# A two-block transformer step on one core: every product whose sum nobody reads is left out

## Chip, cores and metric

The kernel is one program on one core of a Trainium2 chip. The metric is the device time of one execution in microseconds, from three executions of the kernel before. The five engines of the core are TensorE (PE, with its weight loads PEld), VectorE (DVE), ScalarE (ACT), GpSimd (POOL) and SyncE (SP), which issues the weight loads from memory. Activations between the stages stay in SBUF; the weights, about 305 MB, are read once.

## What is computed

A sequence of 256 rows of width 1024 goes through two blocks of two layers each, all in float32. Cut to what matters:

```python
# first block: two layers
for layer in range(2):
    x = x + 0.5 * swiglu(rms_norm(x), w_gate, w_up, w_down)            # f0, f2
    h = rms_norm(x, mix_norm[layer])
    x = x + (diff_stickbreak_mixer(h) if layer == 0 else mla_mixer(h))  # m0, m1
    x = x + memory_cross_attention(rms_norm(x), rms_norm(mem))          # c0, c1
    x = x + 0.5 * swiglu(rms_norm(x), w_gate, w_up, w_down)            # f1, f3
# second block: two layers
for l in range(2):
    h = x @ w_in[l]
    mix = concat([gla(h), rwkv7(h), nsa(h)]) @ w_out[l]
    x = layer_norm(ALPHA * x + mix)                                     # b0, b1
    x = layer_norm(ALPHA * x + swiglu(x))                               # f4, f5
```

None of the products that the change leaves out appears in this text. They multiply the 128x128 identity by itself, and their sums are overwritten unread.

## The kernel before

The work is cut into twelve stages that run one after the other: `f0 m0 c0 f1 f2 m1 c1 f3 b0 f4 b1 f5` (`STAGES`). The `f` stages are feed-forward layers, `m0` and `m1` the two mixers of the first block, `c0` and `c1` its cross attentions, `b0` and `b1` the mixers of the second block. In the trace `m0` and `c0` lie about between 205 and 450 us, `m1` and `c1` between 822 and 1070, `b0` between 1240 and 1560, `b1` between 1755 and 2080; what lies between these stretches is feed-forward.

Every stage is a list of pieces. A piece has a name and a number, and each engine has a function that does its part of it, so the list of pieces is the order of the work on all engines alike. Each engine runs its part in that order and waits on semaphores where it needs another engine's result. In an `f` stage the list is written by a few loops. In the six other stages (`m0 c0 m1 c1 b0 b1`) it is woven from chains: a chain is a list of pieces that follow each other, each chain has a letter, and the string of the stage in the table `WEAVE` (line 40) says letter by letter from which chain the next piece comes (`woven`, line 1204).

The letter `z` is one chain more. Its pieces are called "warm", and TensorE alone does them. The code is (lines 334 and 3092)

```python
    def idle_banks(self, pe):
        return [self.ps[b] for b, key in self.holder.items() if pe.knows(*self.at("evicted", key))]

def pe_warm(e, K):
    for b in K.idle_banks(e)[0:1]:
        e.mm(b[:, 0:128], K.ident, K.ident, True, True, free=True)
```

So a warm piece is one float32 product of the identity (tile `consts`) with itself, 128x128 by 128x128, into a bank of PSUM whose last content TensorE knows to be read already. It waits for nothing and signals nothing. Where no bank is known to be free it is nothing at all: the strings have 1009 `z`, and the program has 955 such products. A float32 product of this size is two rows MATMUL and two LDWEIGHTS in the trace, so the group `ps<-consts 128*128 128x128` with 1912 rows is these 955 products and one more.

What else the prediction's steps touch:

- Weights come in units of up to 1024 columns. SP loads a unit into one of six places of `ring`. ACT copies it to `w_hi` (`act_splits`, the value rounded to float32r), DVE writes the rest to `w_lo` (`dve_splits`), and TensorE multiplies with both. There are four places for such pairs; ACT waits until TensorE has used the pair before.
- Activations are split in the same way: `h` holds hi and lo halves, and `x` is the residual stream.
- A linear layer (`pe_lin`) is a run of products `ps<-w_hi,h` and `ps<-w_lo,h`, or `ps<-h,w_hi` and `ps<-h,w_lo` in the feed-forward layers.
- At the end of a stage the parts of `x` are finished one by one: DVE adds the sum, ACT and DVE split it into the next stage's `h` (`act_x`, `dve_x`), POOL squares it and adds the squares in `rows` (`pool_x`). TensorE's first linear layer of the next stage waits for the parts in turn, and in its middle for POOL's squares (`pe_rs`, products `ps<-consts,rows`).
- Head norms are chains on DVE: a reduction, some fifteen small operations on `stats`, and the multiplications (`act_head_squares`, `dve_head_norm`). TensorE then turns the result (`tr`, line 145, `ps<-consts,scratch`).

Of the kernel before, what the change touches and what calls it, by code (L numbers as in the profile page):

```python
# [37 lines left out]


WEAVE = {  # L40
    "b0": ("zzzzzzzzzrzzrrrrrgzgzgrhlzhzhzzzzrzzzhzzzzzzzrzzhrzzzhzgzzhzzzzzzzhzzzzzzzzhzzhzzzzzzzzzzrzzzzzz"
           "zzzzhhrhzzzzzzzhzzzzzzlzhzzzzhzrrrzzhzrlhzhzzrrzszzzhzrzsrzzzhzzzsszhzzzzzszzszzzzznzzzzzzzzzzrz"
           "rzzzzzzzzsrnznzrzzzzzzrznzzzzzzzznnnzzzzzzzzzznzzwzzzzzzzzzzzzzzzzzzzzzrzzzzzzzzzzzzzzzzvrsvrrnz"
           "zzzzzzrzzrnrnzrzzzzzzzzzzzrwzzrurnrsunsuwvsrsbsusrvrrruzvbrvrarvrwbabuwurwaawrauramurzvzwbuabzbv"
           "awzzbumabummzmzzzmmmmmmmzmmmmzzzzzzzzzzzmmzzmzmmmmmmzmzmzmzzmzzzzzzzzmzzzmzzzzzmmmmzzzz"),
    "b1": ("zzzzzzzzzzrzrrgrzgrgrhgzzrrlhzzzzzzzzzzzzzzzzzzzzzhhzzzrzzzrzzhhzzhzzzzzzzzzzzzzzzzzzzzzzzzzzzzz"
           "zzzzzzzzzzzzzrhhhzzrzzhzzhzzzzzzlzzzrzzrzzzzzzzzzzzrrhhzrshzzhzsrzzlsszhrhszzrhzrrhrzhsrhzzzzzzz"
           "zzszrzzzzszrzzznrzszzzzzznzrsnrzzznzznzzzzzznrrrnwzzzzzzzzzzzzzzzzzzzzzzznzzzzzzzzzzruzzzzzzzzzz"
           "zzzzzzzzzzzzzzzzzrsrwnzrznzszzszzrsrzzrrnzrrnrnrzurvrwwbuavrrvmrvzzrvzzzzazbubvwbauawwuaubwvauab"
           "buvuwvazbuambummmzzzzmzmmmmmmzmzzzzmmmzmmmmmmmmzzzzmzzzmzzzzzmzmzzmzmzzzzmzzzzmzmzzzzmzzm"),  # L50
    "c0": ("zzzzzzzzzpppzzzzpzzzzzzzzzzzzzzzzzzzzzzzzzzzzzzzzzzzzzzzzzzzpzpazcbacdbzacdbdozozzzozoozoozzozoo"
           "zzzzzzozozzzzzzzzzzzozzzzzzzzz"),
    "c1": ("zzzzzpppzzzpzzzzzzzzzzzzzzzzzzzzzzzzzzzzzzzzzzzzzzzzzzppazbdazbcdabcdcozzoozozozzooozozzzoozzzzz"
           "zzzzzzzzzzzzzzzoozzzz"),
    "m0": ("zzypzzzzzqqzzzzzqzzzzzzzzkzkqzzpzzzzzzzzzzzzzzzzkyzzzzzzykbakyqlycvaycvbaabcacbcaacctbsbatscaacc"
           "tassactszczssotzystzztssyzzzootsttotstoozzozzzzzzzzozzoozozoozoozzzzzozoozzzzzz"),
    "m1": ("zyzpzzzzzqqzqzkkqzyzqyzzkzqqzqkzzzqkzzzzzzzzzzzzzzzzzzzzzzzzzzzzzzzzkzzzzzzzzzzzzzzzzzzzzzzzzzzz"
           "zzzzzzzzzzzzzkzzzzzzhzzzzzzzzzzzzzzzzzyzzzzzzzyzttzzttzzzzyztzzzzzzzzzttztzzzzzzzzzzzzzuzuzyuayu"
           "zuucauducbadacbedacbedbacaebcodaceabcbedadebecdzaobedaeoozozzzozoozoooooozozzzzozozzzzzzzzzzzzzz"
           "z"),  # L60
}

# [3170 lines left out]
```

How the kernel before makes its waits and increments, by code:

```python
    def wait_ge(self, sem, n):  # L114
        if self.e is not None and self.covered.get(id(sem), 0) < n:
            self.e.wait_ge(sem, n)
            self.covered[id(sem)] = n
# [8 lines left out]
    def then(self, ins, kind=None, key=None):  # L126
        if kind is None:
            self.n_own += 1
            sem, n = self.K.S.sem(self.own), self.n_own
            ins.then_inc(sem, 1)
        else:
            ins.then_inc(*self.up(kind, key))
            sem, n = self.K.S.at(kind, key)
        self.wait_ge(sem, n)
# [187 lines left out]
    def bank(self, pe, ring, key):  # L323
        i = self.cursor.get(ring, 0)
        self.cursor[ring] = i + 1
        b = ring[i % len(ring)]
        if b in self.holder:
            pe.wait_ge(*self.at("evicted", self.holder[b]))
        self.holder[b] = key
        self.where[key] = b
        return self.ps[b]
# [43 lines left out]
def act_splits(e, K):  # L376
    while e.next_split < len(K.pairs):
        u = K.pairs[e.next_split]
        before = K.pairs[u.pair - NU] if u.pair >= NU else None
        if u.piece > e.piece + 1 and not can_split(e, K, u, before):
            return
        assert before is None or before.piece <= e.piece, (u.n, u.piece, e.piece)
        if before is not None:
            e.wait_ge(*K.used(before))
        e.wait_ge(*K.loaded(u))
        e.act(u.his, u.src, ACT.Copy).then_inc(*e.up("split_hi", u.n))
        e.next_split += 1
# [2 lines left out]
def dve_splits(e, K):  # L391
# [5 lines left out]
            return  # L397
        if before is not None:
            e.wait_ge(*K.used(before))
        e.wait_ge(*K.loaded(u))
```

## Time and profile before

| | |
|---|---|
| runs of the kernel before | 2283.53, 2286.56, 2306.3 us |
| median | 2286.56 us |
| span of the profiled execution | 2285.3 us |
| instructions in the span | 36711 |
| TensorE busy | 2202.2 us, 96% |
| VectorE busy | 1526.7 us, 67% |
| ScalarE busy | 1104.3 us, 48% |
| GpSimd busy | 418.3 us, 18% |
| mean granted TensorE clock | 0.988 |

The span is the time from the first to the last instruction of one profiled execution. The page gives no other time for that execution; the span is 1.3 us under the median. Busy is the time in which an engine has at least one instruction in work. The end of a product on TensorE is modelled and laps over the start of the next by some 0.2 us, so a run of equal products is measured best from its start to the start of what follows it. The granted clock is 1.00 where TensorE runs at 2.4 GHz and 0.50 at 1.2 GHz.

### The profile page before, as it was taken

How to read it: one execution, taken by the hardware profiler on the slowest of the kernel's cores; microseconds unless marked ns; L12 is line 12 of the kernel's file. 1: busy time of each engine (PE TensorE's matmuls, PEld its weight loads, DVE VectorE, ACT ScalarE, POOL GpSimd, SP SyncE). 2: the span in 40 equal slices, each digit the busy share in tenths (PEclk: the TensorE clock that was granted, in tenths of full speed). 3: DMA queues.
4: the chain of work that ended last, by engine and by line, in shares of the span. 5: the costliest groups of instructions: out<-in, count | busy, mean ns of one | idle time of the engine just before them, and what ended most of it. 6: DMA issues, size and time to landing. Idle time of an engine off the chain costs nothing.

```text
span 2285.3 us, 36711 instructions
## 1 busy us (share of the span) xinstructions
PE 2202.2 (96%) x14388; PEld 1953.8 (85%) x14388; DVE 1526.7 (67%) x2709; ACT 1104.3 (48%) x1997; POOL 418.3 (18%) x379
## 2 busy tenths in 40 slices
PE   6999999999999999999999998999998999999997
PEld 5888888988888888999888987889887988788886
DVE  5976765587678667756876685456766586456765
ACT  4654454365456544535654522346555432345554
POOL 2521001122112100012220030101213123101223
PEclk9999999999999999999999999999999999999999
DMA  6545432254555443133544321114544320303552
GB/s 242 192 170 173 148 130 74 74 192 182 180 194 190 177 157 133 38 111 130 188 179 174 139 85 61 57 38 152 186 181 149 133 94 1 116 29 127 187 178 90
DMA packets 88444, 310.32 MB, mean 136 GB/s; under 512 B 9808, under 2 KB 11600, under 8 KB 87760
## 3 DMA queue, kind: packets, MB, share of 16 engines
q1 hardware_dynamic: 87984, 305.29, 37.5%
q8 instruction: 114, 1.87, 0.3%
q10 hardware_dynamic: 288, 2.69, 0.3%
q14 instruction: 58, 0.48, 0.1%
HBM read 306.89 MB, written 1.05 MB: 135 GB/s over the span
## 4 chain that ended last, share of the span: by engine, by line
PE 91%; DVE 4%; ACT 2%; DMA 1%; issue 1%; POOL 0%; SPq 0%; DVEq 0%; ACTq 0%; POOLq 0%
PE ps L140 89%; PE ps L145 2%; DVE scratch L165 2%; DMA ring<-in_w 1%; ACT w_hi L154 1%; DVE w_lo L165 1%; ACT scratch L154 0%; DVE x L165 0%; DVE scratch L192 0%; DVE stats L182 0%; POOL scratch L165 0%; ACT scratch L191 0%; DVE scratch L177 0%; DVE scratch L171 0%; SPq L207 0%
## 5 line engine op out<-in xcount | busy, mean ns | idle before, releaser
L165 DVE TENSOR_TENSOR w_lo<-ring,w_hi 128x1024 fp32r<-128x1024 f32 (+2 forms) x571 | 694.2, 1230 | 420.0 <-ACT w_hi L154 414.3
L140 PE MATMUL ps<-h,w_hi 128*128 128x512 f32 (+1 forms) x2784 | 872.2, 372 | 24.0 <-DVE h L177 19.1
L154 ACT ACTIVATE w_hi<-ring 128x1024 fp32r<-128x1024 f32 (+2 forms) x571 | 581.5, 1032 | 487.0 <-PE ps L140 485.4
L140 PE MATMUL ps<-h,w_lo 128*128 128x256 f32 x2448 | 688.0, 281 | 0.0
L140 PEld LDWEIGHTS ps<-h,w_hi 128*128 128x128 f32 x2784 | 504.2, 190 | 123.3 <-issue 21.4
L140 PEld LDWEIGHTS ps<-h,w_lo 128*128 128x128 f32 x2448 | 465.0, 190 | 0.0
L140 PE MATMUL ps<-f,w_hi 128*128 128x512 f32 (+1 forms) x1444 | 419.2, 356 | 3.2 <-DVE f L165 3.2
L140 PE MATMUL ps<-f,w_lo 128*128 128x256 f32 x1184 | 331.9, 280 | 0.0
L165 POOL TENSOR_TENSOR f<-f_work,f 128x256 fp32r<-128x256 f32 x132 | 187.7, 1422 | 596.2 <-ACT f L154 596.1
L140 PEld LDWEIGHTS ps<-f,w_hi 128*128 128x128 f32 x1444 | 254.4, 189 | 46.1 <-DVE w_lo L165 3.6
L140 PE MATMUL ps<-scratch 128*128 128x128 f32 (+9 forms) x1952 | 256.3, 300 | 8.7 <-DVE scratch L192 2.5
L140 PE MATMUL ps<-consts 128*128 128x128 f32 x1912 | 246.5, 280 | 0.0
L140 PEld LDWEIGHTS ps<-consts 128*128 128x128 f32 x1912 | 233.5, 195 | 10.3 <-issue 6.1
L140 PEld LDWEIGHTS ps<-scratch 128*128 128x128 f32 (+4 forms) x1952 | 210.4, 186 | 33.0 <-issue 10.7
L140 PEld LDWEIGHTS ps<-f,w_lo 128*128 128x128 f32 x1184 | 223.9, 189 | 0.1
L191 ACT ACTIVATE scratch<-ps 128x512 f32<-128x512 f32 (+9 forms) x203 | 98.5, 499 | 221.7 <-PE ps L140 171.8
L140 PE MATMUL ps<-w_hi,h 128*128 128x512 f32 (+2 forms) x528 | 161.2, 380 | 0.1
L165 POOL TENSOR_TENSOR rows<-x 128x256 f32<-128x256 f32 x64 | 40.7, 636 | 589.5 <-DVE x L165 583.1
L165 DVE TENSOR_TENSOR f_work<-f_work,ps 128x256 f32<-128x256 f32 x306 | 126.6, 415 | 3.6 <-ACT f_work L191 3.5
L165 POOL TENSOR_TENSOR scratch<-scratch 128x512 f32<-128x512 f32 (+1 forms) x69 | 87.9, 1276 | 201.1 <-DVE scratch L165 83.6
L165 DVE TENSOR_TENSOR f_work<-f_work 128x256 f32<-128x256 f32 x264 | 113.8, 431 | 8.6
L140 PEld LDWEIGHTS ps<-w_hi,h 128*128 128x128 f32 x528 | 98.8, 190 | 15.9 <-issue 1.2
(136 smaller groups left out, 2136.4 us busy)
## 6 DMA issues: line engine op xcount, KB each, us to landing
ring<-in_w SPq DMA_DIRECT2D x520, 512.0 KB, 3.3
ring<-in_w SPq DMA_DIRECT2D x48, 384.0 KB, 3.4
ring<-in_w SPq DMA_DIRECT2D x16, 396.0 KB, 4.8
stage_consts<-in_ctwo ACTq DMA_DIRECT2D x1, 1344.0 KB, 5.9
stage_consts<-in_cthree ACTq DMA_DIRECT2D x1, 1281.0 KB, 6.8
stage_consts<-in_cone SPq DMA_DIRECT2D x1, 1083.0 KB, 5.7
x<-in_x SPq DMA_DIRECT2D x4, 256.0 KB, 4.4
scratch<-in_m SPq DMA_DIRECT2D x1, 1024.0 KB, 6.7
```

What stands on the lines that cost most here:

```text
L140: return self.e.matmul(out, lhsT, rhs, start=start, stop=stop, skip_group_check=free)
L145: return self.e.transpose(out, x, self.K.ident[0:x.shape[0], 0:x.shape[0]])
L154: return self.e.activation(out, x, func, **k)
L165: return self.e.tensor_tensor(out, a, b, op)
L191: return self.e.activation(out, a, ACT.Copy)
```

## The change

All `z` are taken out of the six strings. No other letter moves. The program keeps every other product and every wait; the order of DVE, ACT, POOL and SP is row for row the same (1984, 1536, 167 and 114 rows). On TensorE 955 float32 products go. Of the table one stage stands for all:

```diff
-    "c0": ("zzzzzzzzzpppzzzzpzzzzzzzzzzzzzzzzzzzzzzzzzzzzzzzzzzzzzzzzzzzpzpazcbacdbzacdbdozozzzozoozoozzozoo"
-           "zzzzzzozzzzzzzzzzzzozzzzzzzzz"),
+    "c0": ("ppppppacbacdbacdbdoooooooooo"
+           "ooo"),
```

In the pieces of TensorE's order below, `ps` is a PSUM bank, `h`, `w_hi` and `w_lo` are activations and split weights, `scratch` is the working area, `consts` in a product of its own is the identity, and "waits" names the semaphores that stand before an instruction.

TensorE in `c0`, after the query projection (before: from 405.75 us):

```order
 L140 MATMUL ps<-w_lo,h 128x512
 L140 MATMUL ps<-w_hi,h 128x512
-L140 MATMUL ps<-consts 128x128 x47
 L145 MATMUL ps<-consts,scratch 128x128 [waits normed_dve]
 L145 MATMUL ps<-consts,scratch 128x128 x3
```

Forty-seven products go between the last product of the projection and the turning of the normed queries, which waits for DVE's head norm.

TensorE in `m1`, around the head norm of the queries (before: from 885.85 us):

```order
 L140 MATMUL ps<-w_lo,h 128x512
 L140 MATMUL ps<-w_hi,h 128x512
-L140 MATMUL ps<-consts 128x128 x32
 L140 MATMUL ps<-w_hi,h 128x512 [waits split_lo_dve,evicted_act,evicted_dve]
 L140 MATMUL ps<-w_lo,h 128x512
@@ -4294,5 +4263,4 @@
 L140 MATMUL ps<-w_lo,h 128x512
 L140 MATMUL ps<-w_hi,h 128x512
-L140 MATMUL ps<-consts 128x128 x40
 L140 MATMUL ps<-w_hi,h 128x512 [waits split_lo_dve,evicted_act,evicted_dve]
 L140 MATMUL ps<-w_lo,h 128x512
```

The two projections on either side move together; each still waits for banks that ACT and DVE empty.

TensorE in `b1` (before: from 1834.83 us and from 1845.40 us):

```order
 L145 MATMUL ps<-consts,scratch 128x128 [waits evicted_dve]
 L145 MATMUL ps<-consts,scratch 128x128 x3
-L140 MATMUL ps<-consts 128x128 x21
 L140 MATMUL ps<-scratch,stage_consts 128x512 [waits pairs_pool,evicted_act]
-L140 MATMUL ps<-consts 128x128 x3
 L140 MATMUL ps<-scratch,ring 128x256 [waits sigmoid_act,loaded4]
 L140 MATMUL ps<-scratch,ring 128x256 x3
@@ -8243,5 +8122,4 @@
 L140 MATMUL ps<-scratch 128x128 [waits scaled_dve,evicted_dve,evicted_act]
 L140 MATMUL ps<-scratch 128x128 x3
-L140 MATMUL ps<-consts 128x128 x44
 L140 MATMUL ps<-scratch,stage_consts 128x512 [waits squares_dve]
```

Here 21, 3 and 44 products go; the waits on ACT, DVE, POOL and the weights stay where they were.

In all, 16 such runs have 21 to 47 products, 475 together; the other 480 products stand in shorter runs.

## Rows read from the trace of the kernel before

**Rows 1.** The page: busy time of each engine.
```profile
PE 2202.2 (96%) x14388; PEld 1953.8 (85%) x14388; DVE 1526.7 (67%) x2709; ACT 1104.3 (48%) x1997; POOL 418.3 (18%) x379
```

**Rows 2.** The page: the chain that ended last, by engine.
```profile
PE 91%; DVE 4%; ACT 2%; DMA 1%; issue 1%; POOL 0%; SPq 0%; DVEq 0%; ACTq 0%; POOLq 0%
```

**Rows 3.** Groups of instructions: whole span, then 205:450 and 1755:2085 (busy, mean ns, idle before).
```profile
L140 PE MATMUL ps<-consts 128*128 128x128 f32 x1912 | 246.5, 280 | 0.0
...
L140 PE MATMUL ps<-consts 128*128 128x128 f32 x328 | 41.2, 280 | 0.0
...
L140 PE MATMUL ps<-consts 128*128 128x128 f32 x530 | 69.9, 282 | 0.0
```

**Rows 4.** Cores: us from first to last instruction, mean granted TensorE clock.
```profile
core 0: 2285.3 us, clock 0.988
```

**Rows 5.** Timeline of c0 (start us, us, engine, line, operation, [idle before]): PE, then DVE.
```profile
405.75 10.66 PE L140 MATMUL ps<-consts 128*128 128x128 f32 x94
416.25 1.04 PE L145 MATMUL ps<-consts,scratch 128*128 128x128 f32 x8
...
414.25 1.22 DVE L165 TENSOR_TENSOR scratch<-scratch,stage_consts 128x1024 f32<-128x1024 f32 x1
```

**Rows 6.** Timeline, c0 into f1: PE, then DVE.
```profile
442.53 6.41 PE L140 MATMUL ps<-consts 128*128 128x128 f32 x56
448.70 0.47 PE L140 MATMUL ps<-h,w_hi 128*128 128x512 f32 x1
...
452.72 0.59 DVE L177 SCALAR_TENSOR_TENSOR h<-x,consts,h 128x256 fp32r<-128x256 f32 x1 [0.65 <-ACT h L154]
```

**Rows 7.** Timeline of m1: PE, then DVE.
```profile
885.85 7.31 PE L140 MATMUL ps<-consts 128*128 128x128 f32 x64
...
895.75 9.09 PE L140 MATMUL ps<-consts 128*128 128x128 f32 x80
...
886.36 3.35 DVE L182 TENSOR_REDUCE stats<-scratch 128x32 f32<-128x3072 f32 x1 [1.37 <-ACT scratch L154]
...
902.94 0.69 DVE L192 COPY scratch<-ps 128x512 f32<-128x512 f32 x1
```

**Rows 8.** Timeline of b1: PE and DVE at 1835 us, then at 1845 us.
```profile
1834.83 4.85 PE L140 MATMUL ps<-consts 128*128 128x128 f32 x42
...
1835.39 3.67 DVE L165 TENSOR_TENSOR w_lo<-ring,w_hi 128x792 fp32r<-128x792 f32 x4
1840.59 0.69 DVE L165 TENSOR_TENSOR scratch<-ps,scratch 128x512 f32<-128x512 f32 x1 [1.53 <-PE ps L140]
...
1845.40 10.09 PE L140 MATMUL ps<-consts 128*128 128x128 f32 x88
...
1854.39 0.62 DVE L171 TENSOR_SCALAR scratch<-scratch,stage_consts 128x256 f32<-128x256 f32 x2
1855.33 1.02 PE L140 MATMUL ps<-scratch,stage_consts 128*128 128x512 f32 x2
```

**Rows 9.** Waits, whole span, engine waited for (us in total, times, longest): DVE for PE.
```profile
DVE scratch L165 <- PE ps L140: 51.9, 41, 3.5
...
DVE scratch L171 <- PE ps L140: 21.8, 21, 3.3
```

**Rows 10.** Windows (us, busy of PE PEld DVE ACT POOL with counts, PEclk, DMA share, GB/s).
```profile
207.20:210.50 3.30, 0.00 (x0) 0.00 (x0) 2.34 (x5) 1.00 (x1) 0.00 (x0) 1.00 0.87 263
210.60:217.30 6.70, 5.70 (x23) 5.34 (x24) 5.66 (x22) 5.70 (x13) 0.61 (x1) 0.50 0.33 99
...
1330.20:1333.50 3.30, 0.35 (x4) 0.16 (x2) 3.11 (x3) 0.00 (x0) 2.84 (x3) 1.00 0.00 0
1333.60:1336.90 3.30, 3.30 (x11) 2.27 (x11) 0.69 (x1) 0.67 (x2) 0.00 (x0) 0.50 0.02 5
```

**Rows 11.** Timeline of PE in b0.
```profile
1448.64 4.33 PE L140 MATMUL ps<-scratch 128*64 128x256 f32 x40
...
1453.58 2.88 PE L140 MATMUL ps<-scratch 128*64 128x256 f32 x12
```

More of the change, by code:

```diff
@@ L40 @@
 WEAVE = {
[L41 to L50, printed above, removed]
@@ L51 @@
-    "c0": ("zzzzzzzzzpppzzzzpzzzzzzzzzzzzzzzzzzzzzzzzzzzzzzzzzzzzzzzzzzzpzpazcbacdbzacdbdozozzzozoozoozzozoo"
[L52 to L56, printed above, removed]
@@ L57 @@
-    "m1": ("zyzpzzzzzqqzqzkkqzyzqyzzkzqqzqkzzzqkzzzzzzzzzzzzzzzzzzzzzzzzzzzzzzzzkzzzzzzzzzzzzzzzzzzzzzzzzzzz"
-           "zzzzzzzzzzzzzkzzzzzzhzzzzzzzzzzzzzzzzzyzzzzzzzyzttzzttzzzzyztzzzzzzzzzttztzzzzzzzzzzzzzuzuzyuayu"
-           "zuucauducbadacbedacbedbacaebcodaceabcbedadebecdzaobedaeoozozzzozoozoooooozozzzzozozzzzzzzzzzzzzz"
+    "b0": ("rrrrrrgggrhlhhrhrhrhghhhhr"
+           "hhrhhlhhrrrhrlhhrrshrsrhsshssnr"
+           "rsrnnrrnnnnnwrvrsvrrn"
+           "rrnrnrrwrurnrsunsuwvsrsbsusrvrrruvbrvrarvrwbabuwurwaawrauramurvwbuabbv"
+           "awbumabummmmmmmmmmmmmmmmmmmmmmmmmmmmmmmmm"),
@@ new lines @@
+    "b1": ("rrrgrgrgrhgrrlhhhrrhhh"
+           "rhhhrhhlrrrrhhrshhsrlsshrhsrhrrhrhsrh"
+           "srsrnrsnrsnrnnnrrrnwnru"
+           "rsrwnrnssrsrrrnrrnrnrurvrwwbuavrrvmrvrvabubvwbauawwuaubwvauab"
+           "buvuwvabuambummmmmmmmmmmmmmmmmmmmmmmmmmmmmmmmm"),
+    "c0": ("ppppppacbacdbacdbdoooooooooo"
+           "ooo"),
+    "c1": ("ppppppabdabcdabcdcooooooooooo"
+           "oo"),
+    "m0": ("ypqqqkkqpkyykbakyqlycvaycvbaabcacbcaacctbsbatscaacc"
+           "tassactscssotysttssyootsttotstoooooooooooooo"),
@@ L60 @@
+    "m1": ("ypqqqkkqyqykqqqkqkk"
+           "khyyttttyttttuuyuayu"
+           "uucauducbadacbedacbedbacaebcodaceabcbedadebecdaobedaeooooooooooooooo"
            "z"),
```

## The prediction

> **What bounds the kernel now.** I first read the page's busy times: TensorE is busy for 96% of the span, the next engine, VectorE, for 67% [rows 1]. The chain that ended last agrees: 91% of it lies on TensorE [rows 2]. Both figures count the products that the change takes out, so they can't tell by themselves whether TensorE is the bound. The groups of instructions give the size of that part: the products of the identity with itself are busy for 246.5 us, none of it in the feed-forward stretches but for their ends; of the four stretches of the woven stages the first, m0 with c0, has the least, 41.2 us; the last, b1, has 69.9 us; m1 with c1 and b0 have about as much as that [rows 3]. Without them TensorE is busy for about 1955 us of 2285, and the question is what fills the rest. So I read next, in the timeline, what stands on the other engines beside the longest runs of these products, and last where the granted clock fell.
>
> One product costs 0.223 us: 47 of them lie between 405.75 and 416.25 us [rows 5]. The 955 that go are thus 213 us at full clock; the rest of the 246.5 is the overlap of modelled ends and the few that ran at half clock. 213 us is the most that could be saved, 9% of the span, and 0 is the least if the clock stays as it is.
>
> **What the change saves.** A run of these products saves time only where TensorE's next piece was ready before the run's end, and where somebody then waits for that piece. I take the sixteen runs of 21 to 47 products first, 475 products and 106 us. The rows show three kinds.
>
> In the first kind the run covers a wait that stays. In c0 it starts at 405.75 us. DVE's head norm ends at 414.25 + 1.22 = 415.47, and the turning of the queries starts at 416.25, so 0.8 of 10.5 us can be saved [rows 5]. In b1 a run of 44 starts at 1845.40, DVE ends what is waited for at 1854.39 + 0.62 = 1855.01 and TensorE goes on at 1855.33: 0.3 of 9.9 us [rows 8]. At the end of c0 the products run from 442.53 to 448.70, and the parts of x arrive one by one until DVE's last split, which starts at 452.72. TensorE's first layer needs them all and was only about 0.6 us behind the last, so of 6.2 us some 0.6 is saved [rows 6].
>
> In the second kind TensorE's next piece was ready, but the engine that takes its result has no time for it. In m1 the 32 products at 885.85 and the 40 at 895.75 stand beside a head norm that holds DVE from 886.36 without a pause until it copies TensorE's result at 902.94 [rows 7]. If TensorE runs its projection 6 us earlier, the copy still comes at 902.94. Of these 15.9 us at most 1 is saved.
>
> In the third kind somebody waits. In b1 TensorE spends 4.7 us on 21 products from 1834.83. DVE is on weight splits until 1835.39 + 3.67 = 1839.06 and then waits 1.53 us for TensorE [rows 8]. So 1.5 of 4.7 us is saved.
>
> These six runs hold 47 us and save 4.2. The other ten hold 59 us. Read in the same way they give 0.1 to 0.7 us each at the ends of stages and before long waits, and about 2.3 and 2.5 us in two runs of the third kind; together 7. **The long runs save 11 of 106 us.**
>
> The other 480 products, 107 us, stand in some 135 runs of at most 16 products. Most follow work that leaves TensorE's next piece ready. The bounds for them are 0 and 107 us. DVE's waits for TensorE are a second bound: its four largest groups run from 51.9 to 21.8 us and sum to 149 us in the whole span, a part of them in the dense stretches where nothing changes [rows 9]. Between a tenth, as at 442.53, and a third, as at 1834.83, I take 23%: **25 us**. SP, POOL and ACT keep their orders. Their waits get no new companion, and the weights come no earlier than TensorE uses them. ACT fills a new pair when TensorE has used an old one, so where TensorE runs ahead ACT and DVE split earlier, beside the same head norms; this is in the quarter.
>
> **What the change costs.** The granted clock is the other side. From 207.20 TensorE did nothing for 3.3 us; then the clock stood at 0.50, which is 1.2 GHz, for 6.7 us, of which TensorE was busy for 5.7. After 1330.20, where it was busy for 0.35 of 3.30 us, it stood at 0.50 for the next 3.3 us [rows 10]. It also fell with no idle time at all: from 1448.64 TensorE made 40 products of 64 columns in 4.3 us, about 0.11 us apart, and from 1453.58 12 of them took 2.88 us, about 0.24 us apart [rows 11]. Half clock doubles the time of every product. Over the whole span the clock was 0.988 in the mean [rows 4], so 2.4% of the time, some 54 us, was at half clock, in part idle.
>
> Without the long runs TensorE is idle for 4 to 14 us in sixteen places, and as it fell after the empty stretch at 207 it will fall there. Two of these places (those where someone waits and TensorE closes up) I leave out. The two low stretches of [rows 10] are 3.3 and 6.7 us long. TensorE loses half of such a stretch if it works all through it, 1.7 or 3.4 us, and nothing if the stretch lies over the gap or if nobody waits. I take 2.0 us for each of the fourteen, a little over the nearer one: 28 us. In b0 and b1 the short runs thin out as well, among narrow products that let the clock fall even before [rows 11]. I count six more falls of 1.7 us, 10 us, with 0 and 55 us as bounds: the latter if it stays low in all of some 220 us of such stretches, in which half of the time is real work and half of that work is waited for. **Together 38 us**, from 0 to about 100.
>
> The Trainium skill, "TensorE: Matmul & The Clock Gate", Part 1, gives this less weight: for modelling, the penalty of coming up from the low clock is under 1% of a typical kernel's span. One percent here is 23 us, and by it the sum would be about 15 us lower than mine. The trace before already has half clock in 2.4% of its time [rows 4], with these products in place, so I don't rely on it.
>
> **The sum** against the profiled execution's 2285.3 us: 2285.3 - 11 - 25 + 38 = 2287.3. Its span is 1.3 us under the median of the runs, so in terms of the median I say 2288 us: no change that can be told. A measurement of this kernel can tell about 1%, 23 us, from none.
>
> **Rivals.**
> - *The gain stays and the clock hardly falls.* For it: in the chain that ended last TensorE has 91% [rows 2], and in many short runs its next piece was long ready. If half of the short runs' 107 us is saved, and only four new falls of 2 us come, the time is 2285 - 11 - 54 + 8 = 2228. Against it stands m1, where DVE holds everything [rows 7].
> - *Few falls.* The clock falls only after gaps of pure idle time, in ten places at 1.7 us, and the saving is mine: 2285 - 36 + 17 = 2266. Against it: a fall with no idle time [rows 11]. The sentence of the Trainium skill quoted above belongs to this rival.
> - *Slower: in b0 and b1 the clock doesn't come back.* There TensorE does short pieces between waits for DVE. Once at half speed, each piece on the path takes twice as long. This decides if the low level holds over more than about 90 us of the thin stretches in b0 and b1. I price it with its 55 us bound in place of my 10, the long gaps at 28, and a saving of 30: 2285 - 30 + 28 + 55 = 2338. For it: [rows 11]; against it: after 6.7 us of half clock at 217 the full clock was back [rows 10].
> - *The products do something else.* They signal nothing and no engine's order or waits change, so I give this nothing.
>
> **How the numbers follow.** My forecast has 0.40, the fast rival 0.20, few falls 0.12, the slow one 0.28. Few falls lies just inside 1% and spreads to both sides, so half of it, 0.06, counts as faster. Of my forecast's 0.40 I put 0.05 above 1%, since a low clock can only cost more than I counted where it lasts. So faster by over 1% is 0.20 + 0.06 = 0.26, within 1% 0.35 + 0.06 = 0.41, and slower 0.28 + 0.05 = 0.33. For the range I take 2232 to 2340: it holds the two middle cases and the slow rival's price, and ends just inside the fast one's, so that about 0.10 is left out on that side and as much above. My forecast's own range is 2265 to 2310.
>
> **What would show it.** In the profile after: TensorE's busy time falls by about 200 us, less what half clock adds, to some 2000 us. The mean granted clock falls from 0.988 to about 0.96; over 0.98 would speak for the fast rivals, under 0.94 for the slow one. In c0 the turning of the queries starts the same 10.5 us after the projection's end, give or take 1. In m1 DVE's norm and copy stand as before, with TensorE idle beside them. In b1 DVE's wait of 1.53 us is gone. DVE's waits for TensorE fall in the thin stretches if the saving is real and grow if the clock takes it back. I am wrong if the dense feed-forward stretches change their time, or if TensorE's narrow products in b0 and b1 mostly take twice as long.

## The result, and the profile after

In runs that alternated on the same chip the changed kernel takes 2301.7 us in the median of 20 and the kernel before 2291.4 in the median of 20: ratio 1.0047, 95% interval 1.0030 to 1.0064. It is about 11 us slower, half of what I had called distinguishable from nothing, though the interval excludes 1. The profiled execution has a span of 2296.6 us against 2285.3 [rows 4]. (One correction to the section on the change: one `z` is left, the lone last string of `m1`. 956 such products stand in the kernel before, 955 go and one stays; it belongs to the run of 26 that starts at 996.95 us.)

The page of the kernel after: busy times of the engines and the granted clock in 40 slices (a digit is tenths, 9 is 90% or more), then the chain that ended last by engine:

```profile
PE 2059.1 (90%) x12478; PEld 1786.1 (78%) x12478; DVE 1527.0 (66%) x2709; ACT 1104.1 (48%) x1997; POOL 418.7 (18%) x379
...
PEclk9999999899999998889999989799998979799999
...
PE 80%; DVE 12%; ACT 4%; issue 2%; POOL 1%; DMA 1%; SPq 0%; DVEq 0%; ACTq 0%; POOLq 0%
```

DVE, ACT and POOL do the same work in the same time as in [rows 1]. TensorE's busy time falls by 2202.2 - 2059.1 = 143.1 us, where 955 products at 0.223 us were 213. So 70 us of the removed work came back as longer products. In the chain DVE has 12% where it had 4% [rows 2]: the waits for DVE and its norms now show between TensorE's pieces.

The cores view of after, the one group left of [rows 3], and the largest waits of DVE for TensorE (in all, times, longest), which answer to [rows 4, 3, 9]:

```profile
core 0: 2296.6 us, clock 0.940
```

```profile
L140 PE MATMUL ps<-consts 128*128 128x128 f32 x2 | 0.4, 272 | 0.0
```

```profile
DVE scratch L165 <- PE ps L140: 51.7, 38, 3.5
DVE scratch L192 <- PE ps L140: 40.1, 16, 10.8
DVE stats L182 <- PE ps L140: 39.6, 50, 2.6
DVE scratch L171 <- PE ps L140: 28.6, 19, 4.6
```

The first group of waits, 51.9 us before [rows 9], has not moved, and the last has grown from 21.8 to 28.6. The four together grew from 149 to 160 us, so DVE waits for TensorE more than before and not less. The mean clock fell from 0.988 to 0.940. A mean of 0.940 with two levels means 12% of the time at 0.50, some 270 us, where it was 54.

**Where the time went.** Both traces hold the same 12476 other rows of products in the same order, so the same product can be looked up in both. DVE's 2709 rows are the same too. The table has the start after minus the start before, in us: of TensorE's product at the place, and of DVE's row at the same place, which at a stage's end is its last split of x.

| place | start before | TensorE, after - before | DVE, after - before | DVE's step |
|---|---|---|---|---|
| m0 begins | 205.0 | +0.1 | +0.1 | |
| m0 ends, c0 begins | 393.5 | -6.6 | -0.9 | -1.0 |
| c0 ends, f1 begins | 448.7 | -4.2 | +2.8 | +3.7 |
| f1, past its first layer's beginning | 460 | +2.7 | +2.6 | -0.3 |
| f2 ends | 826.1 | -0.4 | -0.4 | -3.0 |
| m1 ends, c1 begins | 1002.7 | -4.0 | +1.8 | +2.2 |
| c1 ends, f3 begins | 1056.9 | -1.3 | +5.8 | +3.9 |
| f3, past its first layer's beginning | 1067 | +5.3 | +5.3 | -0.4 |
| f3 ends | 1240.1 | +5.3 | +5.3 | 0.0 |
| b0 ends | 1556.1 | +6.9 | +6.9 | +1.6 |
| f4 ends | 1763.5 | +5.1 | +5.1 | -1.8 |
| b1 ends, f5 begins | 2083.6 | +9.7 | +11.6 | +6.5 |
| end | 2285.3 | +11.3 | | |

The two columns must be read together. At the end of a stage TensorE now runs ahead into the next stage's first layer, and that lead is worth nothing: the layer needs the parts of x, which DVE finishes one by one. In f1 TensorE comes 4.2 us early, does a few products and then stands idle for 3.28 us until DVE's split, which is 2.8 us late; at f3 it is the same (1.3 us early, 3.27 us idle, DVE 5.8 us late). TensorE's steps of 6.9 and 6.6 us in these two layers are thus a lead that is given back, plus a delay that DVE brought from c0 and c1. The time that lasts is lost in c0 (3.7 us), m1 (2.2), c1 (3.9), b0 (1.6) and b1 (6.5).

```profile
450.05 0.79 PE L140 MATMUL ps<-h,w_hi 128*128 128x512 f32 x1 [3.28 <-DVE h L177]
...
1061.21 0.80 PE L140 MATMUL ps<-h,w_hi 128*128 128x512 f32 x1 [3.27 <-DVE h L177]
```

In c0 and c1 most of it comes at one row. DVE waits there for the first result of the projection, and TensorE runs the projection at half clock behind the idle time that the runs missing at 388.69 and 996.95 left: it waits over 4 us for POOL's squares in the middle of the layer, and what it does next, at 398.40 and 1009.40, is at 0.50. The rows of c0 before and after, then of c1 before and after:

```profile
405.95 0.75 DVE L171 TENSOR_SCALAR scratch<-ps,stats 128x512 f32<-128x512 f32 x1 [1.49 <-PE ps L140]
408.19 0.75 DVE L171 TENSOR_SCALAR scratch<-ps,stats 128x512 f32<-128x512 f32 x1 [4.63 <-PE ps L140]
...
1014.85 0.75 DVE L171 TENSOR_SCALAR scratch<-ps,stats 128x512 f32<-128x512 f32 x1 [1.45 <-PE ps L140]
1019.53 0.75 DVE L171 TENSOR_SCALAR scratch<-ps,stats 128x512 f32<-128x512 f32 x1 [4.31 <-PE ps L140]
```

The waits are 3.1 and 2.9 us longer, and DVE's rows stay late from there to the end of the stage, where short products at half clock add 0.6 and 1.1 us.

Not every step belongs to the change. The long part of a feed-forward stage runs at one of two paces, with the full clock in both. In f1 the kernel before makes 568 rows of products in 100 us, and after makes 579 of the same:

```profile
500.00:600.00 100.00, 100.00 (x568) 86.77 (x567) 74.16 (x114) 54.67 (x96) 24.27 (x18) 1.00 0.49 176
500.00:600.00 100.00, 100.00 (x579) 87.49 (x578) 75.59 (x117) 56.23 (x99) 24.76 (x18) 1.00 0.55 179
```

That is worth 2.8 us in f1 and 3.1 us in f4, where after has the quicker pace too, and it hides that much of what was lost elsewhere. The edit doesn't decide it: e7 and e10 below are one kernel, and f4 took the quick pace in the one and the slow pace in the other. No run shows what decides it.

Some windows of after in which the clock was low (us, busy of PE PEld DVE ACT POOL with counts, PEclk, DMA share, GB/s):

```profile
398.40:405.10 6.70, 6.70 (x20) 5.64 (x21) 4.39 (x15) 1.38 (x2) 0.00 (x0) 0.50 0.48 159
412.10:422.20 10.10, 4.44 (x14) 3.70 (x15) 6.28 (x17) 0.60 (x1) 0.00 (x0) 0.50 0.28 93
449.60:456.30 6.70, 6.25 (x18) 4.57 (x19) 3.95 (x10) 2.03 (x4) 4.91 (x7) 0.50 0.42 139
890.00:907.00 17.00, 5.73 (x14) 4.45 (x15) 14.13 (x11) 0.80 (x2) 0.00 (x0) 0.50 0.19 59
1009.40:1016.10 6.70, 6.11 (x18) 5.18 (x19) 4.79 (x15) 2.04 (x3) 0.54 (x1) 0.50 0.41 143
1060.60:1067.30 6.70, 6.09 (x17) 4.41 (x18) 4.11 (x10) 2.03 (x4) 4.91 (x7) 0.50 0.47 141
1845.70:1866.10 20.40, 9.00 (x44) 5.43 (x44) 13.35 (x26) 4.63 (x12) 0.00 (x0) 0.50 0.25 87
```

The second column (TensorE's busy time) tells how much of such a stretch can cost anything. From 890.00 TensorE was idle for two thirds of 17 us, so the low clock there is mostly free. At 398.40 and 1009.40 it was busy for over 90%, in the two projections whose result DVE waits for. At 449.60 and 1060.60 it was busy as much and did 18 and 17 rows of products, but this cost nothing that lasts, since DVE's parts of x came late anyway: DVE's delay is 2.8 us ahead of the first stretch and 2.6 behind it, 5.8 and 5.3 us for the second. In about the same seven microseconds of f1's first layer the kernel before did 45 at full clock:

```profile
449.00:456.00 7.00, 7.00 (x45) 6.24 (x44) 2.43 (x5) 2.42 (x4) 3.63 (x6) 1.00 0.08 28
```

Next, the timeline of after at the places of [rows 5 to 8]: c0, the entry of f1, m1, b1 (PE rows, then DVE rows; in brackets the idle time before).

```profile
398.35 1.86 PE L140 MATMUL ps<-consts,rows 128*128 128x1 f32 x8 [4.18 <-POOL rows L165]
...
407.77 0.39 PE L140 MATMUL ps<-w_hi,h 128*128 128x512 f32 x1
417.76 1.97 PE L145 MATMUL ps<-consts,scratch 128*128 128x128 f32 x8 [9.61 <-DVE scratch L165]
...
444.49 0.40 PE L140 MATMUL ps<-h,w_hi 128*128 128x512 f32 x1
...
887.11 0.39 PE L140 MATMUL ps<-w_hi,h 128*128 128x512 f32 x1
901.27 0.79 PE L140 MATMUL ps<-w_hi,h 128*128 128x512 f32 x1 [13.78 <-DVE scratch L192]
...
1847.63 2.05 PE L140 MATMUL ps<-scratch,stage_consts 128*128 128x512 f32 x2 [4.44 <-DVE scratch L165]
1859.91 2.08 PE L140 MATMUL ps<-scratch,stage_consts 128*128 128x512 f32 x2 [9.08 <-DVE scratch L171]
```

```profile
455.56 0.58 DVE L177 SCALAR_TENSOR_TENSOR h<-x,consts,h 128x256 fp32r<-128x256 f32 x1 [0.65 <-ACT h L154]
...
883.95 3.35 DVE L182 TENSOR_REDUCE stats<-scratch 128x32 f32<-128x3072 f32 x1 [1.37 <-ACT scratch L154]
...
900.53 0.69 DVE L192 COPY scratch<-ps 128x512 f32<-128x512 f32 x1
...
1840.41 4.55 DVE L165 TENSOR_TENSOR w_lo<-ring,w_hi 128x792 fp32r<-128x792 f32 x4
...
1844.88 0.68 DVE L165 TENSOR_TENSOR scratch<-ps,scratch 128x512 f32<-128x512 f32 x1
...
1849.71 0.69 DVE L171 TENSOR_SCALAR scratch<-ps 128x512 f32<-128x512 f32 x1 [1.76 <-PE ps L140]
```

The rows of the kernel before that answer to 1847.63 and 1849.71:

```profile
1843.72 1.10 PE L140 MATMUL ps<-scratch,stage_consts 128*128 128x512 f32 x2 [0.20 <-DVE scratch L165]
1844.86 0.69 DVE L171 TENSOR_SCALAR scratch<-ps 128x512 f32<-128x512 f32 x1 [0.82 <-PE ps L140]
```

They show the three kinds of run again. At 398.35 TensorE, 5.1 us ahead of before, waits 4.18 us for POOL's squares and has 0.9 left; then its clock is 0.50 for 6.7 us. In m1 DVE's reduction and its copy of TensorE's result stand 16.58 us apart as before (883.95 and 900.53; 886.36 and 902.94 [rows 7]), and TensorE is idle for 13.78 us beside them. At f1 the first product starts 4.2 us earlier (444.49 for 448.70), but DVE's last split of x stands at 455.56 where it stood at 452.72 [rows 6]: 2.8 us late, as all of DVE's rows since the middle of c0. In b1 DVE's copy at 1844.88 no longer waits for TensorE, but little of that is kept. The four weight splits before it took 4.55 us instead of 3.67, one of them alone 1.86 instead of 0.98. Then TensorE's product at 1847.63 ran at half clock (2.05 us instead of 1.10), and DVE waited 1.76 us for it instead of 0.82. DVE's delay against before is 5.0 us at the head of this stretch, 4.3 at 1844.88, and 4.9 at 1849.71.

### The profile page after: what moved, and what is told of

The parts are those of the page before. It is cut to its first block, busy times and chain, and to the rows that moved or that the text cites. A ratio compares the mean times of both kernels' runs of the same rounds, so it can differ in the third digit from the quotient of the medians.

```text
span 2296.6 us, 32891 instructions
## 1 busy us (share of the span) xinstructions
PE 2059.1 (90%) x12478; PEld 1786.1 (78%) x12478; DVE 1527.0 (66%) x2709; ACT 1104.1 (48%) x1997; POOL 418.7 (18%) x379
## 4 chain that ended last, share of the span: by engine, by line
PE 80%; DVE 12%; ACT 4%; issue 2%; POOL 1%; DMA 1%; SPq 0%; DVEq 0%; ACTq 0%; POOLq 0%
PE ps L140 78%; DVE scratch L165 5%; DVE w_lo L165 3%; PE ps L145 2%; ACT w_hi L154 2%; ACT scratch L154 1%; DMA ring<-in_w 1%; DVE scratch L192 1%; DVE stats L182 1%; DVE x L165 1%; POOL scratch L165 1%; POOL rows L165 0%; ACT h L154 0%; DVE stats L177 0%; DVE h L177 0%
## 5 line engine op out<-in xcount | busy, mean ns | idle before, releaser
L140 PE MATMUL ps<-h,w_hi 128*128 128x512 f32 (+1 forms) x2784 | 881.1, 375 | 39.9 <-DVE h L177 25.7
L140 PEld LDWEIGHTS ps<-h,w_hi 128*128 128x128 f32 x2784 | 510.7, 192 | 143.2 <-issue 32.7
L140 PEld LDWEIGHTS ps<-h,w_lo 128*128 128x128 f32 x2448 | 470.6, 192 | 0.0
L140 PE MATMUL ps<-scratch 128*128 128x128 f32 (+9 forms) x1952 | 278.6, 320 | 49.3 <-DVE scratch L165 29.4
L140 PEld LDWEIGHTS ps<-scratch 128*128 128x128 f32 (+4 forms) x1952 | 229.3, 202 | 85.4 <-issue 34.1
L140 PE MATMUL ps<-w_hi,h 128*128 128x512 f32 (+2 forms) x528 | 169.2, 396 | 18.0 <-DVE scratch L192 13.8
L140 PEld LDWEIGHTS ps<-w_hi,h 128*128 128x128 f32 x528 | 104.1, 200 | 39.0 <-DVE scratch L192 14.2
L145 PE MATMUL ps<-consts,scratch 128*128 128x128 f32 (+2 forms) x544 | 90.2, 307 | 47.6 <-DVE scratch L165 35.1
L145 PEld LDWEIGHTS ps<-consts,scratch 128*128 128x128 f32 (+2 forms) x544 | 70.5, 153 | 61.5 <-DVE scratch L165 35.0
```

The source lines that it names most:

```text
L140: return self.e.matmul(out, lhsT, rhs, start=start, stop=stop, skip_group_check=free)
L145: return self.e.transpose(out, x, self.K.ident[0:x.shape[0], 0:x.shape[0]])
```

## The experiments

Ten kernels were run. A product that is kept or dropped is a `z` in `WEAVE`; nothing else differs unless told. Each ratio is to the kernel before, run in turn on the same chip; a clock without more words is the mean of the profiled execution. In the strings of all ten kernels those 53 `z` that made no product in the kernel before are missing too.

### e1 and e2: long runs only, short runs only

In e1 the 16 long runs (475 products) stay and the short ones go; in e2 the 481 products of the short runs stay. The string of c0 before, in e1, and (behind the dots) in e2:

```diff
-    "c0": ("zzzzzzzzzpppzzzzpzzzzzzzzzzzzzzzzzzzzzzzzzzzzzzzzzzzzzzzzzzzpzpazcbacdbzacdbdozozzzozoozoozzozoo"
-           "zzzzzzozozzzzzzzzzzzozzzzzzzzz"),
+    "c0": ("zzzzzzzzzpppzzzzpzzzzzzzzzzzzzzzzzzzzzzzzzzzzzzzzzzzzzzzzzzzppacbacdbacdbdoooooooozoozzzzzzozozz"
+           "zzzzzzzzzozzzzzzzzz"),
...
+    "c0": ("ppppppazcbacdbzacdbdozozzzozoozoozzoooooo"),
```

> The sixteen runs of 21 to 47 identity products stand as before (475 products), the 480 shorter-run ones are gone. Theory S (small terms, as predicted): the short runs cost 25 us of waiting and the falls of the clock that they prevent cost 10, so the time is before minus 15 us, ratio about 0.993. Theory L (large terms: the trace after shows 276 us at half clock where 56 were before, so both sides are about twice as large): short runs save 45 and cost 25, minus 20 us, ratio 0.991. Theory C (the short runs are what holds the clock in b0 and b1): plus 10 us, 1.004.

> The reverse: the 480 short-run products stay, the 475 of the long runs are gone. Theory S: saves 11, costs 28, so before plus 17 us, ratio about 1.007. Theory L: saves 20, costs 50, plus 30 us, 1.013. Theory C: the long runs cover waits and the clock that falls there falls beside nothing urgent, plus 0 to 5 us, 1.000 to 1.002.

**Measured.** e1: 0.9966 (0.9945 to 0.9988), clock 0.961, but 0.966 to 0.968 in eight of the twelve executions. e2: 1.0048 (1.0030 to 1.0066), clock 0.962. **What follows.** The short runs' removal alone gains about 8 us and the long runs' removal alone costs about 11. The two effects of the change have opposite signs, as the prediction had them. Their sum is +3 us, and together they measure +11. That difference is 0.33%, and the three intervals leave about as much uncertainty on it, so it isn't shown that the two effects don't add up. In e2's trace DVE's rows fall behind at the same two rows as in after, by 2.8 us in c0 and 2.2 in c1, so this loss belongs to the long runs. Here the low clock in the first layers of f1 and f3 costs too, since it lasts beyond DVE's last split: DVE's delay grows by 2.6 and 2.4 us.

In e1's trace TensorE is 11 us ahead of before at 1900 us (6 of them from the quick pace in f1 and f4), 8 at 2000, and 3 behind at 2050. So it is in b1's attention that it loses all. Windows of e1:

```profile
1980.00:1989.80 9.80, 9.80 (x73) 7.80 (x72) 6.07 (x18) 5.33 (x13) 0.00 (x0) 0.84 0.01 3
1990.00:2020.50 30.50, 30.46 (x109) 21.66 (x108) 7.80 (x27) 8.33 (x29) 0.00 (x0) 0.50 0.00 1
2020.70:2030.00 9.30, 8.67 (x57) 6.69 (x57) 6.94 (x27) 4.74 (x17) 0.00 (x0) 1.00 0.00 0
```

For 30.5 us the clock stood at 0.50 while TensorE was busy all the time; these are small products, 3.6 per us where the next stretch has 6.1. This was the slow rival's mechanism, in one place. The executions of e1 with a clock of 0.966 to 0.968 can hardly have had this stretch: 30 us more at half clock lower the mean of such an execution by 0.007.

### e3: only what somebody waits for

```diff
-    "m0": ("zzypzzzzzqqzzzzzqzzzzzzzzkzkqzzpzzzzzzzzzzzzzzzzkyzzzzzzykbakyqlycvaycvbaabcacbcaacctbsbatscaacc"
-           "tassactszczssotzystzztssyzzzootsttotstoozzozzzzzzzzozzoozozoozoozzzzzozoozzzzzz"),
+    "m0": ("ypqqqzzkkqpzzzzzzkyzzzzzzykbakyqlycvaycvbaabcacbcaacctbsbatscaacctassactscssotzystzztssyzzzootst"
+           "totstoozzooooooozoozzzzzozoozzzzzz"),
```

261 products are dropped, those of which the trace of before shows that TensorE's next piece was ready and TensorE was on the chain that ended last. 695 stay.

> Of each run only so many products are taken away as the trace of before shows slack for (TensorE's next waits all released earlier, and TensorE on the chain that ended last): 261 go, 695 stay. No new gap should arise, so the clock should stay near 0.988 and only the saving is left. Theory S: minus 30 us, ratio 0.987. Theory L: minus 50 us, 0.978. If other engines take up the slack at once (DVE's order holds everything): minus 0 to 10 us, 0.996 to 1.000.

**Measured.** 0.9931 (0.9908 to 0.9954), 2276.0 us, clock 0.980. The page of e3:

```profile
PE 2161.8 (95%) x13866; PEld 1905.5 (84%) x13866; DVE 1526.6 (67%) x2709; ACT 1104.3 (49%) x1997; POOL 419.5 (18%) x379
```

**What follows.** No theory on record has this number: 0.9931 lies between those that expected 0.987 or less and the one that expected 0.996 or more. 58 us of products went for 16 us of time, so even of the best quarter of the products 27% of their time is left as a net gain. Falls of the clock were new (0.988 to 0.980, which is some 35 us more at half clock); how the rest divides between them and waits one step further on is not shown.

### e4: the same products, one moving column wide

```diff
-        e.mm(b[:, 0:128], K.ident, K.ident, True, True, free=True)
+        e.mm(b[:, 0:1], K.ident, K.ident[:, 0:1], True, True, free=True)
```

> All 956 products stay in place, each with one column instead of 128 moving through TensorE. The weight loads, which take 0.19 us each and set the pace of a float32 product, stay, so TensorE's order and, at full clock, its time are nearly as before; but hardly any columns move. It measures what a lower clock costs without any saving. Theory S: before plus 38 to 50 us, ratio 1.02. Theory L: plus 90 us, 1.04. If the weight loads alone keep the clock up: ratio 1.000 and a granted clock of 0.98.

**Measured.** 1.0543 (1.0517 to 1.0568), 2416.6 us, clock 0.920. The page of e4 and two of its low windows:

```profile
PE 2334.9 (97%) x14388; PEld 2079.1 (86%) x14388; DVE 1525.8 (63%) x2709; ACT 1104.9 (46%) x1997; POOL 417.7 (17%) x379
```

```profile
1383.40:1414.00 30.60, 29.85 (x144) 28.01 (x144) 22.77 (x30) 4.63 (x11) 8.83 (x7) 0.50 0.08 29
2042.40:2072.80 30.40, 29.22 (x135) 23.37 (x137) 10.71 (x37) 7.38 (x14) 2.14 (x2) 0.50 0.02 2
```

**What follows.** The order, the number of instructions and the waits are those of before, TensorE is busy for 97% of the span, and the clock is lower than with nothing in the gaps. So filling the gaps with instructions isn't what held the clock: the full-width products do it, and the one-column products in the same places don't. One column wide they make the kernel 125 us longer than in full width, 115 more than leaving them out. At full clock they still stand 0.223 us apart, as the wide ones do, so each takes its time in TensorE's order and gives nothing for it. The loss is larger than any theory on record expected (90 us at most).

### e5: the ends of the stages put back

After, with the runs at 388.69, 442.53, 996.95, 1050.77, 1559.7 and 2078.3 us put back (152 products, of which after still has one):

```diff
-    "c0": ("ppppppacbacdbacdbdoooooooooo"
-           "ooo"),
+    "c0": ("zzzzzzzzzppppppacbacdbacdbdoooooooozoozzzzzzozozzzzzzzzzzzozzzzzzzzz"),
```

> The changed kernel with six long runs put back, those at the ends of c0, m1's successor, b0, b1 and before c0 and c1 (22, 28, 26, 28, 24 and 24 products, before TensorE's first layer of the next stage). In the changed kernel that first layer runs in part at half clock and TensorE is its bound there. Theory S: these six places cost 2.0 us each and save 0.1 to 0.7, so putting them back gives 9 us: ratio to before about 1.001. Theory P (the price of a fall depends on what follows; before a dense layer that TensorE bounds it is 3 us or more, elsewhere little): 18 us or more back, ratio 0.997 or less. If the falls are paid elsewhere: no change from the changed kernel, 1.005.

**Measured.** 1.0013 (0.9991 to 1.0035), clock 0.949, against 1.0047 for after. **What follows.** Some 8 us of the loss go, which is the number of theory S (2.0 us for each place) and not that of the theory in which a fall before a dense layer costs 3 us or more. The two intervals still overlap a little, so the size is rough. In the trace the steps of TensorE from c0's and c1's end to 500 and 1100 us are 0.4 and 0.0 us, where in after's trace they were 6.3 and 6.6. But DVE's rows show where the time came back: in c0 the delay grows by 0.6 us instead of 3.7, in c1 by 1.5 instead of 3.9, and the wait for c0's projection is what it was in the kernel before:

```profile
406.41 0.75 DVE L163 TENSOR_SCALAR scratch<-ps,stats 128x512 f32<-128x512 f32 x1 [1.49 <-PE ps L132]
```

So the runs at 388.69 and 996.95, which stand ahead of the projections of c0 and c1, account for most of it. The runs at 442.53 and 1050.77 were put back together with them; no run has one kind alone.

### e6: 23 short-run products of b1's attention left out of the kernel before

```diff
...
-           "buvuwvazbuambummmzzzzmzmmmmmmzmzzzzmmmzmmmmmmmmzzzzmzzzmzzzzzmzmzzmzmzzzzmzzzzmzmzzzzmzzm"),
+           "srwnrnssrsrrrnrrnrnrurvrwwbuavrrvmrvrvabubvwbauawwuaubwvauabbuvuwvabuambummmmmmmmmmzmzzzzmmmzmmm"
+           "mmmmmzzzzmzzzmzzzzzmzmzzmzmzzzzmzzzzmzmzzzzmzzm"),
```

> The kernel before, with only the 23 products of the short runs between 1972 and 2056 us in b1 (attention steps, 5 us of products in 84 us) taken out. Theory S: saves a quarter, 1.2 us, and costs at most one fall, 1.7 us: ratio 1.000. Theory H (at half clock such a stretch does not get its full clock back by itself, as in the profile of e1, where the clock was 0.50 for 31 us from 1990): plus 5 to 11 us, ratio 1.002 to 1.005, with a long stretch at 0.50 in the profile.

**Measured.** 1.0035 (1.0015 to 1.0055), yet its profiled execution has a span of 2286.7 us and a clock of 0.987, as before has. The clocks of the single executions resolve this: that one had 0.987, the nine others 0.977 to 0.983, at 2294.9 to 2304.2 us. Of 71 executions of the kernel before, run beside these experiments, nine had 0.982 or less, and these are the nine longest, 2300.0 to 2304.8 us; all others took under 2298. **What follows.** The same products in the same order can be run with two outcomes some 12 us apart, and without these 23 products the longer one comes in nearly all executions. The traces of e1, e7 and e10 show it as a stretch of 30.5 us at half clock in b1's attention, which costs 11 us in each of them; such a stretch lowers the mean clock by 0.007, about as found in the nine executions here (0.977 to 0.983 where the tenth had 0.987). That the kernel before goes the same way, in one execution of eight, is read from its mean clocks and times alone: none of those executions has a trace, and none of the nine of e6 has one.

### e7 and e10: 32 products of m1 left out of the kernel before

The run of 32 at 885.85, which DVE's norm covers [rows 7]. Both are the same kernel; e7 is one execution, e10 is twelve.

```diff
-    "m1": ("zyzpzzzzzqqzqzkkqzyzqyzzkzqqzqkzzzqkzzzzzzzzzzzzzzzzzzzzzzzzzzzzzzzzkzzzzzzzzzzzzzzzzzzzzzzzzzzz"
-           "zzzzzzzzzzzzzkzzzzzzhzzzzzzzzzzzzzzzzzyzzzzzzzyzttzzttzzzzyztzzzzzzzzzttztzzzzzzzzzzzzzuzuzyuayu"
+    "m1": ("ypzzzzzqqzqzkkqzyzqyzzkzqqzqkzzzqkkzzzzzzzzzzzzzzzzzzzzzzzzzzzzzzzzzzzzzzzzkzzzzzzhzzzzzzzzzzzzz"
+           "zzzzyzzzzzzzyzttzzttzzzzyztttztzzzzzzzzzzzzzuzuzyuayuzuucauducbadacbedacbedbacaebcodaceabcbedade"
...
```

> The kernel before, with only the run of 32 products at 885.85 us in m1 taken out. Prediction: DVE's head norm holds until it copies TensorE's result at 902.94, so the projection starts 6 us earlier and what follows the next run starts within 0.5 us of where it did; the time stays, 0 to 1 us less. The rival, that the release moves with TensorE: 6 us less from there on.

> The kernel before without the 32 products that start at 885.85 us in m1, timed this time. Its one execution before this was 10.9 us longer in the trace, all of it between 2000 and 2050 us, in b1, 1100 us behind the place of the edit. Theory (that was one of the executions in which the clock stays low in b1's attention, which the kernel before has as well in about one of seven; the 32 products themselves are hidden behind DVE): ratio 0.999 to 1.001, and about as many executions with a mean clock under 0.983 as the kernel before has. Rival (the edit itself costs a fall of the clock that shows later): 1.003 or more, with the mean clock at 0.981 in most executions.

**Measured.** In e7 TensorE runs its next piece 6.0 us earlier and is only 0.8 us ahead at 904.6, behind DVE's copy. The span was 2296.2 all the same; the 11 us lie between 2000 and 2050, 1100 us behind the edit. e10: 0.9989 (0.9969 to 1.0009), eleven of twelve executions with a clock of 0.984 to 0.987 and one with 0.978. That one happened to be the profiled one, and its windows show the stretch of e1 again, at the same products:

```profile
1990.00:2004.70 14.70, 14.70 (x121) 12.31 (x120) 6.78 (x20) 5.67 (x14) 0.00 (x0) 0.88 0.03 11
2004.90:2035.40 30.50, 30.50 (x112) 22.48 (x112) 7.80 (x27) 7.75 (x27) 0.00 (x0) 0.50 0.00 1
2035.60:2045.00 9.40, 9.40 (x64) 7.35 (x63) 6.94 (x26) 5.29 (x18) 0.00 (x0) 1.00 0.01 2
```

The kernel before, in its profiled execution, at those products:

```profile
1989.90:2020.60 30.70, 30.25 (x201) 23.78 (x199) 15.30 (x48) 14.41 (x43) 0.00 (x0) 0.91 0.01 2
```

**What follows.** The 32 products are hidden: of 7.1 us of TensorE's work 0.8 us is left behind DVE's copy, 3.4 us at half clock right behind it (from 903.6 in e7) take that back, and twelve executions show no gain that their interval of 0.2% could tell. And one trace alone would have blamed this edit for 11 us that have nothing to do with it.

### e8: half as many products, denser

```diff
-        e.mm(b[:, 0:128], K.ident, K.ident, True, True, free=True)
+        i = K.ident.bitcast(mybir.dt.bfloat16)
+        e.mm(b[:, 0:512].rearrange("p (a k) -> p a k", a=2), i[:, 0:128], bc(i, 2), True, True, free=True)
```

523 of these stand in the place of the 956.

> Every second identity product is gone, and each of the other 523 is one bfloat16 product of 512 moving columns, which takes TensorE about 0.22 us like the float32 one of 128 columns it replaces. So half of the time of these products goes, and the columns that move per product are four times as many. Theory L (what the products cost is the place they take on TensorE, what they give is the clock): the saving is half of the whole, 15 to 30 us, and the clock stays at 0.98 or over: ratio 0.990. If the clock asks for busy time rather than for columns: granted clock 0.96 and ratio 1.000 to 1.005.

**Measured.** 1.0003 (0.9980 to 1.0026), clock 0.967, inside the second expectation and outside the first. Windows of e8 in m1, ahead of the fall and in it:

```profile
889.00:898.00 9.00, 4.41 (x21) 1.80 (x20) 8.83 (x7) 1.09 (x2) 0.00 (x0) 0.99 0.00 0
897.90:904.50 6.60, 3.71 (x9) 2.94 (x10) 5.63 (x7) 0.00 (x0) 0.00 (x0) 0.50 0.24 79
```

**What follows.** Half as many products don't fill the gaps: beside m1's norm TensorE was busy for 4.41 of 9.00 us, and the clock fell. What they save on one side they lose on the other, as after does. Together with e4, where TensorE was busy for 97% at a clock of 0.920, the result doesn't bear out the reason that the second expectation gave, though its numbers came true. Whether as many of them as in before would hold the clock as well isn't known; it wasn't tried.

### e9: trimmed, with 31 products put back

e3 with 31 more products, ahead of the places where its clock fell and before's did not (7 in m1, 3 in b0, 21 in b1 before 1843 us). The string of m1, e3 and e9:

```diff
-    "m1": ("ypqqzqzkkqyqykzqqzqkzqkzzzzzzzzzzzzzzzzzzzzzzzzzzzzzzzzkzzzzzzzzzzzzzzzzzzzzzzzzzzzzzzzzzzzzkhzy"
-           "yzttzzttzzzzyztttztzzzzzzzzzzzzzuzuzyuayuzuucauducbadacbedacbedbacaebcodaceabcbedadebecdaobedaeo"
-           "oozzzooooooooozozzzzozozzzzzzzzzzzzzzz"),
+    "m1": ("ypqqzqzkkqyqykzqqzqkzqkzzzzzzzzzzzzzzzzzzzzzzzzzzzzzzzzkzzzzzzzzzzzzzzzzzzzzzzzzzzzzzzzzzzzzkhzy"
+           "zzzzzzzyzttzzttzzzzyztttztzzzzzzzzzzzzzuzuzyuayuzuucauducbadacbedacbedbacaebcodaceabcbedadebecda"
+           "obedaeooozzzooooooooozozzzzozozzzzzzzzzzzzzzz"),
```

> The trimmed kernel with 31 of the removed products put back, ahead of the places where its clock fell and before's did not (7 in m1 before 926 us, 3 in b0 before 1409, 21 in b1 before 1843 us of before's time). Theory (each product's worth is read from its place: it saves 0.22 us if somebody waits, and costs a fall of the clock if it stood in a thin stretch): the falls in the trimmed kernel's b1 at 1822 and at 917 go, 5 us of half-clock time each, while at most 2 to 3 us of waiting come back: ratio 0.990 to 0.993, mean clock 0.983 or more. Rival (the falls come by chance and elsewhere if not there; the 31 products only take their time): 0.994 to 0.996 with clock 0.980.

**Measured.** 0.9908 (0.9886 to 0.9929), 2271.4 us in the median of six, all within 2269.2 to 2273.3, clock 0.983 (0.979 to 0.982 in the five others). The page of e9, and its window over b1's attention:

```profile
PE 2163.7 (95%) x13928; PEld 1911.0 (84%) x13928; DVE 1526.1 (67%) x2709; ACT 1104.1 (49%) x1997; POOL 419.8 (18%) x379
```

```profile
1989.90:2020.00 30.10, 28.85 (x185) 21.09 (x184) 16.13 (x64) 16.86 (x60) 0.00 (x0) 1.00 0.00 1
```

**What follows.** More work than e3, no more time. e9 beats the kernel before by 0.9%, 21 us, and by the ratios to it also after, by 1.4%. Its interval overlaps that of e3, so that the 31 products gain something on e3 is likely and not shown. That they don't cost the 6.9 us which they take on TensorE is. The low stretch at 1822 us of e3 is gone; the one at 917 came back at 918, against what I expected.

## Why the prediction was right, and where it was not

The forecast was 2288 us, no change that can be told, and the result is no such change: +0.5%, 14 us over my number and inside the range. 5 of the 14 us come from the kernel before, whose median is 2291.4 us in 20 runs and was 2286.6 in three. By its steps:

- **"The long runs save 11 of 106 us", and 14 falls of 2.0 us, 28: +17 us for the long runs alone.** e2 measures about +11, and e5 finds some 8 us for six of the places. Right in sign, a little high. I charged every gap alike, but the cost is paid where somebody waits for what TensorE runs behind the gap: in the projections of c0 and c1, at 3.1 and 2.9 us, and not in the first layers of f1 and f3, where DVE's parts of x were late anyway. In m1 and b1 the low clock beside DVE's long chains is mostly idle (5.73 of 17.00 us busy at 890.00), and yet DVE lost 2.2 and 6.5 us over these stages.
- **"23%: 25 us" for the short runs, and 10 us for six more falls: -15 us for the short runs alone.** e1 measures -8. Only the difference of the two terms is measured. For the 10 us being too small speaks the clock: 54 us and six more falls of 3.4 us at half clock would leave 0.984, and most executions of e1 have 0.966 to 0.968. The 23% has no test of its own; e3's 27% is for picked products, and net of new falls.
- **The sum.** My two halves, +17 and -15, are each 6 to 7 us too large in size, and the errors cancel in the sum. That the sum came out right to a few us is in part luck, and the range of 108 us asked for little. What the experiments do bear out is the mechanism: two effects of about one size and of opposite sign.
- **m1.** "The copy still comes at 902.94" beside DVE's norm: 16.58 us apart in both, and e7 with e10 show 32 products worth nothing. Right.
- **c0.** The turning of the queries starts 9.8 us behind the projection's end (the last product starts at 407.77 and takes 0.23 us, the turning starts at 417.76), 10.5 before: inside the 1 us. Right. But projection and turning are both late, by 2.2 and 1.5 us, and that I had not seen.
- **b1.** DVE's wait of 1.53 us is gone: the row at 1844.88 has no idle time before it. Right as a sign, but the saving that I counted from it is not there: 0.7 us is left at that row and 0.2 at 1849.71, and at the next result of TensorE (1856.46 before, 1862.09 after) DVE is 0.6 us later than it was at the head of the stretch.
- **DVE's waits.** I said that they fall if the saving is real and grow if the clock takes it back. They grew, from 149 to 160 us in the four largest groups.
- **The signs of being wrong.** "The dense feed-forward stretches change their time": behind its first layer f3 kept its time to 0.1 us; f1 and f4 became 2.8 and 3.1 us shorter, by a pace that differs between executions of one kernel too. "Narrow products in b0 and b1 mostly take twice as long": the mean clock is 0.90 over b0 and 0.88 over b1, so a fifth to a quarter of these stages is at half clock, not most.
- **TensorE's busy time and clock.** I said some 2000 us and 0.96; it is 2059.1 and 0.940, the very edge of what I gave to the slow rival. The products grew by 70 us at half clock against about 11 that I had allowed for. The time moved by 11 us only, so most of the 70 must be hidden, for the same reason for which the products were hidden: TensorE waits for others there. The term that was mis-sized is thus the number of falls; their price on the path is nearer to what I counted.
- **The rivals.** The gain does not stay (2228) and the falls are not few (2266). The low clock in b1's thin stretches (2338) exists, as e1, e7 and e10 show, but in one place of 30.5 us for about 12 us, not over 90. The profiled execution of after doesn't have this stretch. The Trainium skill, "TensorE: Matmul & The Clock Gate", Part 1, puts the penalty of coming up from the low clock under 1% of a typical span. By it the sum would have been about 2273. The runs don't agree with it for this kernel when its gaps are badly filled: e4 has the order and the number of products of the kernel before, a clock of 0.920, and takes 5.4% longer. For the kernel before itself no run has the price; 54 us at half clock can cost half of that at most, 27 us or 1.2%, as an estimate.
- **Additivity.** I summed long and short runs. Alone they measure +11 and -8, together +11. The missing 8 us are at the edge of the noise. The time at half clock does add up: 120 us more in e2, 93 more in e1 without its stretch of 30.7 us, and 219 more in after.

So the change takes out two kinds of product, and the result is near nothing because both were of about one size: some on which someone waited, some that held the clock. e9 drops the first and keeps the second. What stays open is the share of each place: from one execution to another of the same kernel the steps of a trace move by b1's 12 us and by the 3 us of a feed-forward stage's pace, and only e6 and e10 were timed for a single place.

## What to carry to other kernels

Idle-looking work on TensorE has two prices, and both are read from its place: it costs time where the next piece was ready and somebody waited for it, and it earns time where the next real piece would run at 0.50 and somebody waits for its result. Drop it in the first kind of place and keep it in the second (here above all before the projections of c0 and c1); keeping all was 0.9% and dropping all 1.4% worse than sorting them. To find the place where time is lost, follow the engine that waits, not the one that runs ahead: TensorE's own starts pointed at f1 and f3, DVE's at c0 and c1. Before one trace's difference is blamed on an edit, compare the mean clocks of all executions: the same kernel can have two.
